# A two-layer encoder: the output projection's last columns by token halves, the second norm's two halves placed around them, and the first gate/up products and operand sums in another order

## What is computed

```python
def swiglu(h, w_gu, w_down):
    gu = h @ w_gu
    gate, up = jnp.split(gu, 2, axis=-1)
    return (jax.nn.silu(gate) * up) @ w_down
...
    for l in range(DEPTH):
        h = rms_norm(x, attn_norm[l])
        x = x + hybrid_mixer(h, w_in[l], qk_gain[l], rpb[l], sink[l], out_gain[l], w_out[l])
        h = rms_norm(x, ffn_norm[l])
        x = x + swiglu(h, w_gu[l], w_down[l])
```

## Time and profile before

| | |
|---|---|
| median of 3 runs | 2760.2 us (2759.16 to 2764.7) |
| the profiled execution | 2755.93 us, its span 2754.2 us |
| busy: PE / DVE / ACT / POOL | 94% / 63% / 40% / 20% of the span |
| mean granted TensorE clock | 0.979 of full |
| longest wait of PE by releaser | DVE XN, 51.0 us in 4 waits |
| end of the projection to product (6,0) | 47.20 us in layer 1, 46.98 in layer 2 |

### The profile page before, as it was taken

The page is one execution under the profiler, slowest core; times in us unless marked ns, Lnnn a source line. Parts: engine busy times, 40 slices in busy tenths (PEclk is TensorE's granted clock), DMA queues, the critical chain, the costliest instruction groups (busy, mean ns, idle before and its releaser), DMA issues. The chain is left out here.

```text
span 2754.2 us, 38015 instructions
## 1 busy us (share of the span) xinstructions
PE 2594.8 (94%) x12976; PEld 2165.7 (79%) x12976; DVE 1739.4 (63%) x3390; ACT 1096.0 (40%) x2154; POOL 562.1 (20%) x521
## 2 busy tenths in 40 slices
PE   5999899989799999999979999999897999999997
PEld 5987788778588888878878878878685888888786
DVE  4288667663655555689844986666626555556897
ACT  3333655552522222334343346555525222223342
POOL 2000311110154444300000003111001545442000
PEclk9999999999899999999999999999999999999999
DMA  5211610003122222432232115000221322216123
GB/s 166 76 46 38 153 39 19 12 30 121 62 92 85 77 85 58 150 137 81 73 123 68 45 58 139 25 13 12 97 66 65 100 79 82 77 47 242 45 92 119
DMA packets 230942, 219.84 MB, mean 80 GB/s; under 512 B 54768, under 2 KB 191984, under 8 KB 230768
## 3 DMA queue, kind: packets, MB, share of 16 engines
q1 hardware_dynamic: 222864, 217.61, 24.8%
q10 hardware_dynamic: 7904, 0.04, 0.2%
HBM read 171.87 MB, written 45.73 MB: 79 GB/s over the span
## 5 line engine op out<-in xcount | busy, mean ns | idle before, releaser
L1997 PE MATMUL psum<-OPH_t,WH 128*128 128x512 f32 x704 | 274.9, 391 | 6.6 <-DVE WL L1541 4.8
L1997 PE MATMUL psum<-OPH_t,WL 128*128 128x512 f32 x704 | 274.3, 390 | 0.0
L1997 PE MATMUL psum<-OPL_t,WH 128*128 128x512 f32 x704 | 274.2, 390 | 0.0
L1541 DVE TENSOR_TENSOR WL<-RAW,WH 128x512 fp32r<-128x512 f32 x132 | 160.7, 1217 | 156.8 <-ACT WH L1078 156.8
L963 ACT ACTIVATE T<-T,G 128x192 f32<-128x192 f32 (+4 forms) x352 | 176.7, 503 | 197.5 <-DVE G L1294 194.2
L1804 PE MATMUL psum<-BH,AH 128*128 128x512 f32 x616 | 243.5, 395 | 8.1 <-DVE BL L1609 7.6
L1806 PE MATMUL psum<-BH,AL 128*128 128x512 f32 x616 | 242.4, 394 | 0.0
L1805 PE MATMUL psum<-BL,AH 128*128 128x512 f32 x616 | 242.4, 393 | 0.0
L1997 PE MATMUL psum<-OPH_b,WH 128*128 128x512 f32 x528 | 209.5, 397 | 15.5 <-ACT P1S L1118 8.5
L1430 DVE COPY PT<-psum 128x256 f32<-128x256 f32 (+3 forms) x254 | 105.4, 415 | 176.7 <-PE psum L1911 175.8
L1895 PE MATMUL psum<-QK,QS 128*128 (+5 forms) x576 | 214.6, 463 | 2.0 <-DVE G L1294 2.0
(11 more groups left out here) (197 smaller groups left out, 5724.6 us busy)
## 6 DMA issues: line engine op xcount, KB each, us to landing
RAW<-in_w_gu SPq DMA_DIRECT2D x176, 256.0 KB, 3.8
WDS<-in_w_down SPq DMA_DIRECT2D x88, 256.0 KB, 2.6
UR<-in_w_in SPq DMA_DIRECT2D x56, 256.0 KB, 3.3
g_mid<-GRES SPq DMA_DIRECT2D x28, 512.0 KB, 2.6
WDK<-in_w_down SPq DMA_DIRECT2D x44, 256.0 KB, 7.2
x_res<-X SPq DMA_DIRECT2D x2, 4096.0 KB, 13.7
PR<-in_w_out SPq DMA_DIRECT2D x32, 256.0 KB, 3.6
X<-x_res SPq DMA_DIRECT2D x2, 4096.0 KB, 14.2
```

The costliest lines, as they stand in the source:

```text
L1541: v.tensor_tensor(WL[i][:, :, :], w_source(i, j), WH[i][:, :, :].bitcast(F32), ALU.subtract).then_inc(w_lo, 1)
L1997: last = t.matmul(dst[:, :], w[i][:, k, :], h[o][:, k, :], start=(i in (1, 5, 6) and k == 0 and part == 0), stop=(i in (2, 3, 4) and k == ...
```

## The change

- **Last columns by halves.** Chunk 3 runs eight pieces for row tiles 0 to 3 (`last_columns(0, k)`), then the same eight pieces for tiles 4 to 7. Since the pieces must be kept for both, pieces 28 to 31 get tiles PH2 and PL2 of their own. POOL's first weight sums share their addresses and so wait for the chunk's end (`moved` 60).
- **First half of the norm beside the second half.** DVE adds tiles 0 to 3 and scales them; PE turns them inside the second half (`turn(0, 0)` after k = 3, `turn(0, 4)` after k = 5). XN1 holds four tiles only.
- **Second half of the norm beside the first products.** ORDER starts (1,0), (1,1), both with b11; PE turns tiles 4 to 7 behind them (`turn(1, 0)`, `turn(1, 4)`), then (2,0), (2,1). (6,1) is now ahead of (7,0), so (7,0), (4,0), (3,0) stand together. SLOT gives (1,1) and (2,0) each other's weight tiles.
- **Sums and operands.** The order of operands is b11, b21, t1, t2, t3, t4, b22. t3 moves from POOL to DVE. t2 goes to a tile XT2 of its own, and t4 is taken from XT2.
- Addresses: b11 and b22 change places, AH and AL move with b11, four of GLB's tiles become GLD.

```diff
-        XN1 = at_kb("XN1", [P, MT, D], F32, 152)
+        XN1 = at_kb("XN1", [P, MT // 2, D], F32, 152)
+
+        PH2 = [at_kb(f"PH2_{i}", [P, 512], F32R, kb) for i, kb in enumerate((148, 150, 108, 110))]
+        PL2 = [at_kb(f"PL2_{i}", [P, 512], F32R, kb) for i, kb in enumerate((216, 218, 112, 114))]
...
-                if needed(piece_done(p - 4)):
+                if needed(piece_done(p - 4)) and p < 28:
                     act.wait_ge(moved, piece_done(p - 4))
+                elif p >= 28:
+                    act.wait_ge(piece_lo, p - 3)
...
-            ORDER = [(1, 0), (2, 0), (1, 1), (2, 1), (5, 0), (6, 0), (5, 1), (7, 0), (6, 1), (4, 0), (3, 0), (7, 1), (1, 2),
+            ORDER = [(1, 0), (1, 1), (2, 0), (2, 1), (5, 0), (6, 0), (5, 1), (6, 1), (7, 0), (4, 0), (3, 0), (7, 1), (1, 2),
                      (4, 1), (3, 1)]
...
+                def ffn_squares(half):
+
+                    act.wait_ge(sumsq_act, 12 + 4 * half)
+                    if half:
+                        act.wait_ge(xt_s, 24)
+                    for m in range(4 * half, 4 * half + 4):
+                        act.wait_ge(x_add, 8 + m + 1)
+                        a.activation(XN1[:, m % 4, 512:D], X[:, m, 512:D], ACT.Square,
+                                     accum_out=sumsq[:, m:m + 1]).then_inc(sumsq_act, 1)
...
-                weight_hi(0)
+                a.activation(warm[:, :], eps[:, :], ACT.Sqrt)
+                ffn_squares(0)
+                ffn_root(0)
                 for j in range(4):
                     ffn_input(j)
                 operand_hi("b11")
-                weight_hi(1)
+                weight_hi(0)
                 for j in range(4, 8):
                     ffn_input(j)
+                weight_hi(1)
+                ffn_squares(1)
+                weight_hi(2)
+                keep_first(0)
+                ffn_root(1)
                 operand_hi("b21")
+                weight_hi(3)
+                keep_first(1)
                 for j in range(8, 16):
                     ffn_input(j)
...
+                pool.wait_ge(moved, 60)
                 weight_sums(0)
-                pool.wait_ge(hf_s, 16)
-                pool.wait_ge(t_sum, 1)
-                g.tensor_tensor(op_source("t3"), HF[:, 4:8, 512:S], HF[:, 0:4, 512:S], ALU.subtract).then_inc(t3_sum, 1)
                 weight_sums(1)
...
+                for k in range(KD):
+                    last_columns(0, k)
+                for k in range(KD):
+                    last_columns(1, k)
+                    if k == 3:
+                        turn(0, 0)
+                    elif k == 5:
+                        turn(0, 4)
...
                 for n in range(PRODUCTS):
+                    if n == 0:
+                        pe.wait_ge(hf_s, 8)
+                    elif n == 2:
+                        turn(1, 0)
+                        turn(1, 4)
                     gate_up_product(n)
```

More of the change, by code:

```diff
@@ L598, in op_source @@
             def op_source(o):
-                k0, hf = {"b11": (0, 0), "t1": (0, 0), "b21": (4, 0), "t4": (4, 0), "t3": (0, 1), "b22": (4, 1), "t2": (4, 1)}[o]
+                if o == "t2":
+                    return XT2[:, :, :]
+                k0, hf = {"b11": (0, 0), "t1": (0, 0), "b21": (4, 0), "t4": (4, 0), "t3": (0, 1), "b22": (4, 1)}[o]
                 return HF[:, k0:k0 + 4, 512 * hf:512 * hf + 512]
@@ L1168, in _, with norm @@
                 v = nc.vector
-                def norm(n, gain, hb):
-                    for half in range(2):
+                def norm(n, gain, hb, halves=(0, 1), between=None):
+                    for half in halves:
                         h4 = slice(4 * half, 4 * half + 4)
@@ L1618, in add_product @@
                         last.then_inc(x_sum, 1)
+                add_out(3, range(4))
+                norm(1, g_ffn, 24, (0,))
+                operand_lo("b11")
                 weight_lo(0)
-                operand_lo("b11")
                 weight_lo(1)
+                add_out(3, range(4, MT))
+                norm(1, g_ffn, 24, (1,), lambda: weight_lo(2))
                 operand_lo("b21")
+                weight_lo(3)
                 dve.wait_ge(hf_s, 12)
@@ L1962, in _, with last_columns, turn @@
                 moving(2, 512, 16, None)
-                moving(3, 512, None, lambda m: pe.wait_ge(x_add, m + 1))
-                norm(1, 24)
+                def last_columns(half, k):
+                    p = 24 + k
+                    pe.wait_ge(piece_lo, p + 1)
+                    for m in range(4 * half, 4 * half + 4):
+                        if k == 0:
+                            pe.wait_ge(x_add, m + 1)
+                        ins = three(bank[m][:, :], HH[:, k, P * m:P * m + P], HL[:, k, P * m:P * m + P],
+                                    *piece_parts(p), k == 0, k == KD - 1)
+                        if k == KD - 1 or half and m == MT - 1:
+                            ins.then_inc(moved, 1)
+                def turn(half, k0):
+                    pe.wait_ge(xn_dve, 6 + 4 * half + 4)
+                    for k in range(k0, k0 + 4):
+                        b = 4 * half + k % 4
+                        if k >= 4:
+                            pe.wait_ge(hf_s, 8 * half + k - 3)
+                        else:
+                            pe.wait_ge(x_add, 8 + b + 1)
+                        for i in range(4):
+                            last = t.transpose(bank[b][:, P * i:P * i + P], XN1[:, i, P * k:P * k + P], ident[:, :])
+                        last.then_inc(xt_s, 1)
+                for k in range(KD):
[6 more added lines that the diff above has]
+                        turn(0, 4)
                 def bank_free(i, j):
@@ L1996, in gate_up_product @@
                         for part, (w, h) in enumerate(((WH, OPH), (WH, OPL), (WL, OPH))):
-                            last = t.matmul(dst[:, :], w[i][:, k, :], h[o][:, k, :], start=(i in (1, 5, 6) and k == 0 and part == 0),
+                            last = t.matmul(dst[:, :], w[SLOT[i, j]][:, k, :], h[o][:, k, :], start=(i in (1, 5, 6) and k == 0 and part == 0),
                                             stop=(i in (2, 3, 4) and k == 3 and part == 2), skip_group_check=True)
```

128 lines of the change are left out of this document (73 added, 55 removed).

## The result

The changed kernel takes 2735.75 us (median of 4 runs, 2731.43 to 2738.01), beside 2759.68 for the kernel before (4 runs, 2757.49 to 2764.7): ratio 0.9908, 95% interval 0.9895 to 0.9921. That is 23.9 us faster, against a forecast of 2742 with a range of 2729 to 2751.

What follows compares the result with a forecast made beforehand. TensorE was taken as the bound, with only idle time at the projection-to-products seam winnable. 2755.9 - 2 x (11.2 - 2.5) = 2738.5, or 2742.8 on the median's level; with XN perhaps free, 2742 was forecast, range 2729 to 2751.

Steps and rivals of the forecast that it cites:

- First half hidden, no wait at (1,0): At the projection's end: the 4.17 us wait before the transposes goes, and (1,0) starts at 709.33 without waiting.
- the walk: Step-by-step timing from the last projection columns to (4,0): gain 11.2 us per layer, 22.4 in all, before clock loss.
- Turnings: First-half transposes inside the projection's second half: 32 cost PE 4.6 us, sixteen take 2.3 to the next start.
- The new wait before the second turning: Before the second half's transposes: late root and XN held by GpSimd make PE wait 3.4 us, 2.1 if not held.
- VectorE sets the pace: From HF 15 to (4,0): DVE's closed queue makes products wait 0.7 to 3.2 us, (4,0) longest.
- Clock: Half clock behind the waits before the second transposes and (4,0): 1.0 and 1.5 us, 2.5 per layer.
- RAW for (1,2): At (1,2): tile RAW, asked for when weight 10 is done, arrives in time with 1.3 us of cover.
- (a): The seam goes as walked through: gain 12 to 25 us, 2735 to 2748; chance 0.74.
- (b): GpSimd's sums fall where DVE is idle or hold nothing: gain up to 33 us, 2727 to 2734; chance 0.09.
- (c): RAW, or the first half's norm or pieces, come late: 4 us per layer handed back, 2748 to 2754; chance 0.09.
- (d): The seam's waits only move: no change within 5.5 us, 2755 to 2765; chance 0.04.
- (e): Slower: the clock does not come back between the new waits, 4.9 us per layer, 2770; chance 0.04.

Runs made afterwards that it cites:

- e5: Changed kernel with both turnings of the first half of the tokens moved behind the whole projection: 2746.90 us, ratio 0.9951 to the kernel before.
- e1: Changed kernel with the second norm's root ahead of (2,0)'s high weight part and product 0's copy, the weight's low part behind the norm: 2732.14 us, ratio 0.9891.
- e2: Changed kernel with GpSimd's first four weight sums held back until the last scaling XN is done: 2741.93 us, ratio 0.9925 to the kernel before.
- e4: Changed kernel with operand b22's high and low parts made two steps later, behind (7,0) and U3: 2732.15 us, ratio 0.9898 to the kernel before.
- e7: Changed kernel with the early root and the second half's first sixteen turnings ahead of (1,0), the last sixteen ahead of (2,0): 2750.16 us, ratio 0.9969.
- after: The changed kernel itself, against the kernel before: 2735.75 us, ratio 0.9908.
- r_after: The changed kernel run again, unedited, on one chip with two edited versions: 2734.44 us, ratio 0.9905 to the kernel before.
- e3: Changed kernel with the old order restored, (7,0) ahead of (6,1), so (6,1) stands before (4,0): 2734.20 us, ratio 0.9922 to the kernel before.
- e6: Changed kernel with the sum t3 moved back from DVE to GpSimd: 2740.98 us, ratio 0.9946 to the kernel before.
- e8: Changed kernel with both the early root and operand b22 two steps later: 2730.12 us, ratio 0.9910 to the kernel before.
- r_root_b22: Changed kernel with early root and later b22, run again on the chip of the repeated changed kernel: 2724.36 us, ratio 0.9877 to the kernel before.
- e9: Changed kernel with early root, b22 two steps later and (7,0) ahead of (6,1) together: 2724.92 us, ratio 0.9881 to the kernel before.

## Why the prediction was right, step by step

**First half hidden, no wait at (1,0): right.** The 4.17 wait went, no piece is waited for, and the turnings lie where the walk put them. e5 shows that this place carries about half of the gain.

**Turnings: mis-sized, 2.3 per sixteen.** Inside the projection they take 1.91 as listed, 1.66 to the start of the next matmul (695.25 to 696.91). The 2.3 to 2.4 of the earlier trace rows was not PE's own rate: there PE waited for ACT's copies to free banks. In that row the four transposes of one bank start 0.11 apart and the banks follow each other every 0.58, which is ACT's time for a copy. Inside the projection ACT is ahead. (1,0) starts at 709.71 - 1.35 = 708.36 (1.35 is the later start of the stretch) against 709.33 in the walk: 1.0 earlier. The price of half clock for 32 transposes was too low for the same reason: 6.59 stands against 3.82 at the full rate, not against 4.6.

**The new wait before the second turning: right in kind, slightly too long.** 2.86, where I said 3.4 held and 2.1 not held. Both mechanisms are there: the root behind the copy (e1; it costs 1.0, not 2, since the sum of squares is itself held, which the walk did not have), and XN held by GpSimd (e2). One hold costs 1.1 rather than 1.26, and the row e2 gives for "not held" is 1.72, not 2.1. The Trainium skill, "SBUF — State Buffer", section "Who interferes with whom", says that an operation of the tensor_scalar kind can contend with GpSimd, and that one with at most one SBUF input, outside the two-port modes, does not. The traces agree: XN 3.57 or 4.23 against 2.74, U 0.67 to 0.69 throughout.

**VectorE sets the pace: right.** HF 15 ends at 718.86 + 4.73 = 723.59, 722.24 on the walk's scale, against 724.0. From there to (4,0) it is 26.85 where the walk has 27.8: GpSimd's third sum after HF 15 falls largely beside a U addition, which it cannot hold (row at 748.54: 1.16 instead of 0.69, so it held only 0.5). The waits are 1.60, 0.95, 0.84, 1.99, 0.43 and 2.12 for my 1.0, 1.3, 1.4, 2.3, 0.7 and 3.2. In all (4,0) is 2.7 earlier than forecast, 13.9 before the old place instead of 11.2.

**Clock: the term that was too high.** I charged 1.0 behind the turning's wait and 1.5 at (4,0). Behind 2.86 the clock stayed up in both layers. A window behind the wait, PE alone:

```profile
719.00:725.00 6.00, 6.00 (x41) 1.00 0.00 0
```

At (4,0), behind 2.12, it fell, and cost 1.6 and 1.3, near the 1.5 charged; it does so in twelve of the thirteen layers with a wait of that size there (last section), and where e4 shortens the wait the loss is absent. Sum: 11.2 + 2.7 - 1.5 = 12.4 per layer, 24.8, against 17.4 predicted: 2.7 per layer because (4,0) came earlier than in the walk, 1.0 because half clock was charged at two waits and came at one. On the level of the median that turns 2742.8 into 2735.4, beside 2735.75 measured. So the mechanism was right and the gain was forecast three tenths too small; its errors pointed the same way and did not cancel, and the range was wide enough for them.

**RAW for (1,2): right**, no wait there. **Rivals.** The walk (a) is the case that came; 2735.75 lies at its lower end. (b) needs GpSimd's sums to hold nothing, and e2 shows that they hold. (c) falls with the absence of new waits in the first half and before (1,2), (d) with the measured gain. The sums given under (d) were wrong: layer 1 of the kernel before has eight waits of 17.4 in all, not six of 15.2, and the walk's own seven waits sum to 13.3, not 12.9. (e) names a real danger: e5 and e7 show half clock behind waits of 4.36 and 7.55, but here it fell at (4,0) alone and came back within that product.

## What to carry to other kernels

When work is moved beside other work, ask which engine then has a closed queue and what in that queue is not yet needed: here the order of two products and the place of the root moved almost nothing, while postponing one operand by two steps gave 5 us. A closed queue is one in which the engine has no idle time left, so that every operation in it delays all that follow. Take the price of an operation on one engine from a stretch where no other engine paces it. And measure a small change over its own stretch of the trace, beside the medians: the same work ahead of the stretch differed by up to 7.3 us between executions.

## What the chip did that I had not expected

- **The same wait does not always do the same to the clock.** 2.86 before the turning, behind dense work, left the full rate in all ten layers that have it (after, r_after, e3, e4, e6: 32 transposes in 3.82 or 3.83). A wait of 2.12 to 2.17 at (4,0), in the kernel after the last of six within 23 us, was followed by half clock in twelve of the thirteen layers that have it (after, r_after, e1, e5, e6, layer 1 of e2, layer 2 of e7), at once or within the first seven matmuls. Layer 2 of e2 is the exception: its wait is 2.13 and the full rate stayed (its row, and a window from it on: us, PE busy, granted clock 1.00, DMA share, GB/s).

```profile
2107.73 0.47 PE L2082 MATMUL psum<-OPH_t,WH 128*128 128x512 f32 x1 [2.13 <-DVE U L1609]
```

```profile
2107.60:2111.60 4.00, 3.87 (x17) 1.00 0.78 222
```

  It also gives the price, in one kernel: from (4,0) to the last U3 its layers take 391.70 with the half clock and 390.17 without. Where the wait at (4,0) is 0.48 to 1.26 (e3, e4, e8, r_root_b22, layer 1 of e7) the clock stays up there. The size of the wait alone does not decide: 2.68 before (7,0) left the full rate in all four layers that have it (e3, e9), and 1.99 before (6,1) was followed by half clock in layer 1 of e7 (starts 0.43 apart) and in no other layer. In e6 the clock falls within (4,0), from starts 0.23 apart to 0.38 and 0.43:

```profile
751.88 0.59 PE L2082 MATMUL psum<-OPH_t,WH 128*128 128x512 f32 x1
752.26 0.63 PE L2082 MATMUL psum<-OPL_t,WH 128*128 128x512 f32 x1
```

  There is scatter as well: 2.19 in r_root_b22 brought 0.72 over 6 us, and the same 2.18 or 2.19 in e1, e8 and e9 nothing (the 32 transposes take 3.82). No run varies the work before a wait by itself, so that the earlier work is what decides is a reading of these rows and not shown, and the rule behind it stays open.
- **A GpSimd sum of 1.29 us costs VectorE about 1.1 us and is itself listed with up to 3.86**, and even an addition of four columns is held (1.24 instead of 0.16). The rows read as if the two engines took turns: a sum asked for while VectorE is busy ends late (726.95 + 3.20), and VectorE's next operation of two SBUF operands ends late in its turn (728.92 + 3.38).
- **Transposes of 128 x 128 in float32 start 0.11 us apart** when no bank is waited for (sixteen, and the next matmul 1.66 behind the first).
